# Twelve of the 24 gate blocks as seven half-block products instead of eight, and their activation sums on GpSimd, in a hybrid decoder step

## The reference, cut to what matters

```python
u = rms_norm(x, lp['norm_g'][0])
nq, nkv, ngate, sz, sxbc, sdt, dqkv, mg = split_in(u @ lp['w_in'])
...
gates = jax.nn.sigmoid(mg.reshape(B, T, 3, D_MODEL).astype(jnp.float32)).astype(x.dtype)
mix = (gates[:, :, 0] * o_a + gates[:, :, 1] * o_b + gates[:, :, 2] * o_cc) @ lp['w_out']
```

## Time and profile before

| | us |
|---|---|
| median of 3 runs (lowest, highest) | 3270.55 (3268.74, 3283.62) |
| the profiled execution, its own time | 3274.83 |
| its span from the first to the last instruction | 3273.0 |
| state space stage, gate products and scan | about 1006 to 1311 |
| prompt attention stage: head and transposes of keys and queries | 1311 to 1362 |
| prompt attention stage: the 32 steps | 1362 to 1854 |

### The profile page before, as it was taken

One profiled execution on the slowest core, in us unless ns is written; L12 is line 12 of the kernel. 1 busy time (PEld: TensorE's weight loads), 2 busy tenths in 40 slices (PEclk: granted clock), 3 DMA queues, 4 the chain that ended last, 5 costly groups with the idle time before them and its releaser, 6 DMA issues. The chain is left out here.

```text
span 3273.0 us, 42944 instructions
## 1 busy us (share of the span) xinstructions
PE 3015.6 (92%) x15198; PEld 2004.1 (61%) x15198; DVE 1257.5 (38%) x2963; ACT 640.6 (20%) x1529; POOL 469.3 (14%) x351
## 2 busy tenths in 40 slices
PE   7999999989997899699899899899699999989998
PEld 5777777665555565454554565455488888874443
DVE  3111123225642675255555343133456656550000
ACT  2111000002220333233333221144311111110000
POOL 0001000004301432100000100011122332220000
PEclk8999999999998889899999999899799999999999
DMA  7544253428854432621110444200143333404010
GB/s 171 118 95 103 75 166 112 146 84 231 254 160 129 147 103 65 181 69 36 40 32 33 142 138 156 94 15 33 55 141 110 121 136 108 141 22 158 34 34 26
DMA packets 336639, 344.79 MB, mean 105 GB/s; under 512 B 60945, under 2 KB 305361, under 8 KB 335078
## 3 DMA queue, kind: packets, MB, share of 16 engines
q1 hardware_dynamic: 296730, 262.54, 27.6%
q10 hardware_dynamic: 39734, 79.98, 7.2%
HBM read 289.11 MB, written 110.01 MB: 122 GB/s over the span
## 5 line engine op out<-in xcount | busy, mean ns | idle before, releaser
L284 PE MATMUL d_ps<-d_w,mixer_u_T 128*128 128x288 f32 (+2 forms) x2048 | 610.8, 437 | 15.9 <-PEq L145 10.3
L284 PEld LDWEIGHTS d_ps<-d_w,mixer_u_T 128*128 128x128 f32 x2048 | 375.4, 195 | 150.4 <-issue 47.9
L288 PE MATMUL d_ps<-mixer_u_T,d_w 128*128 128x352 f32 x1152 | 428.9, 498 | 24.4 <-ACT d_ob L308 13.8
L2923 PE MATMUL down_ps<-down_w,feed_g_T 128*128 128x512 f32 x704 | 305.4, 596 | 8.4 <-DMA down_w<-ffn_w_down 8.4
L288 PEld LDWEIGHTS d_ps<-mixer_u_T,d_w 128*128 128x128 f32 x1152 | 206.4, 199 | 131.8 <-issue 70.1
L2923 PEld LDWEIGHTS down_ps<-down_w,feed_g_T 128*128 128x128 f32 x704 | 134.4, 191 | 177.7 <-issue 168.5
L3133 PE MATMUL ffn_ps<-up_u_T,up_up_w 128*128 128x264 f32 x704 | 165.2, 394 | 6.3 <-DMA ffn_state<-state_ffn_conv 6.3
L3133 PE MATMUL ffn_ps<-up_u_T,ffn_S 128*128 128x264 f32 x704 | 163.8, 386 | 0.0
L3133 PE MATMUL ffn_ps<-ffn_T,up_up_w 128*128 128x264 f32 x704 | 163.8, 386 | 0.0
L308 DVE COPY d_ob<-d_ps 128x288 f32<-128x288 f32 (+3 forms) x144 | 66.4, 462 | 233.0 <-PE d_ps L284 158.3
L3133 PEld LDWEIGHTS ffn_ps<-up_u_T,up_up_w 128*128 128x128 f32 x704 | 133.8, 193 | 29.5 <-issue 6.7
(11 more groups left out here) (467 smaller groups left out, 3783.0 us busy)
## 6 DMA issues: line engine op xcount, KB each, us to landing
out_dil_sample<-cache_dil_w ACTq DMA_DIRECT2D x10, 3264.0 KB
up_up_w<-ffn_w_up SPq DMA_DIRECT2D x44, 512.0 KB, 5.1
cmp_rows<-cache_nsa_kv SPq DMA_DIRECT2D x128, 128.0 KB
graw<-d_ob SPq DMA_DIRECT2D x72, 176.0 KB
mix_gate<-graw SPq DMA_DIRECT2D x24, 528.0 KB, 6.0
dils_qb<-proj SPq DMA_DIRECT2D x24, 512.0 KB, 6.9
d_w<-w_in SPq DMA_DIRECT2D x24, 512.0 KB, 5.4
ssd_x<-proj SPq DMA_DIRECT2D x29, 384.0 KB, 4.8
```

Source lines behind the costliest of these rows:

```text
L284: mm = pe.matmul(self.ps[u % 2][0:rows, 0:cols], self.u_T[:, k, r0:r0 + rows], self.view(i)[:, k, :], start=(k == 0), stop=(k == DK - 1))
L288: mm = pe.matmul(self.ps[u % 2][:, 0:cols], self.view(i)[:, k, x, :], self.u_T[:, k, c * third:(c + 1) * third], start=(k == 0), stop=(k = ...
L2923: mm = pe.matmul(ps[i % ring][:, 512 * h:512 * (h + 1)], lhs_T[:, k, r0:r0 + m], w[:, k, 512 * h:512 * (h + 1)], start=(k == 0), stop=(k = ...
```

## The change

Six of the twelve gate parts (the first twelve blocks, `PLAIN`) stay as they are and run in the state space stage. The other twelve blocks are done in the prompt attention stage by the new class `Gates`, two blocks (a pair) at a time. The weights of a pair are a matrix of 2 by 2 halves A (row: block, column: half of the 1024 inputs), the activations one of 2 by 2 halves B (row: half of the inputs, column: half of the tokens), and the four half results come from seven products P1 to P7 (the scheme of Winograd and Strassen) instead of eight. Each product is made in two quarters x = 0, 1 of 264 tokens, 4 instructions of TensorE each, into `ps[x]`.

- T0 to T2, sums over the activations (three matrices of 4 x 528 columns), are made once, by 6 instructions of GpSimd in the state space stage (`sums_lane`, from 0.4 to 0.9 of the stage). The fourth, B12, is made in place in `u_T` by VectorE at the start of the attention stage (2 instructions).
- S2, S3, S4 and A21 + A22, sums over weights, are made by 4 instructions of GpSimd for every pair.
- ScalarE copies P1 out (`kept`), VectorE makes all the sums of results from `ps` (14 additions a pair), 8 of them the results that are stored.
- To make room, three tiles of the state space stage and `raw` of the attention stage now lie in other tiles, the square's unused result goes to `yout`, and `oa` has 2 slots instead of 4, with a wait for the store of two heads before.

```diff
+class Gates:
+    ORDER = [(p, x) for p in ("P1", "P2", "P6", "P7", "P5", "P4", "P3") for x in range(2)]
+    RING = 4
...
+        def pool_program(pool):
+            yield
+            for x in range(2):
+                pool.tensor_tensor(self.T_of(0, x), self.B(0, 1, x), self.B(0, 0, x), ALU.subtract).then_inc(self.T_made, 1)
+                yield
+                pool.wait_ge(self.T_made, 3 * x + 1)
+                pool.tensor_tensor(self.T_of(1, x), self.B(1, 1, x), self.T_of(0, x), ALU.subtract).then_inc(self.T_made, 1)
+                yield
+                pool.wait_ge(self.T_made, 3 * x + 2)
+                pool.tensor_tensor(self.T_of(2, x), self.B(1, 0, x), self.T_of(1, x), ALU.subtract).then_inc(self.T_made, 1)
+                yield
...
+        last_reader = dict(P6="C11", P7="U", P5="W", P4="V", P3="C21")
+        def pe_program(pe):
+            for i in range(pairs):
+                pe.wait_ge(self.w_in[i % 2], 32 * (i // 2 + 1))
+                for p, x in ORDER:
+                    if p == "P2":
+                        pe.wait_ge(self.held, 2 * i + x + 1)
+                    elif p != "P1":
+                        pe.wait_ge(self.summed, self.added(i, last_reader[p], x))
+                    elif i:
+                        pe.wait_ge(self.summed, self.added(i - 1, "C12", x))
+                    if p in S_needed:
+                        pe.wait_ge(self.S_made, 4 * i + S_needed[p])
...
+                    for k in range(KH):
+                        mm = pe.matmul(self.ps[x][:, 0:self.quarter], lhs(i)[:, k, :], rhs(x)[:, k, :], start=(k == 0), stop=(k == KH - 1))
...
+                dve.tensor_tensor(out, base, self.ps[x][:, 0:self.quarter], ALU.add).then_inc(self.summed, 1)
...
+        def pool_program(pool):
+            for i in range(pairs):
+                pool.wait_ge(self.w_in[i % 2], 32 * (i // 2 + 1))
+                if i:
+                    pool.wait_ge(self.product, NP * i)
+                pool.tensor_tensor(self.S(3), self.A(i, 0, 0), self.A(i, 1, 0), ALU.subtract).then_inc(self.S_made, 1)
...
-                act.copy(oa[:, r, i * P:(i + 1) * P], O[s % 2][:, :]).then_inc(out_made, 1)
+                if r >= 2 and i == 0:
+                    act.wait_ge(stored, 16 * (r - 1))
+                act.copy(oa[:, r % 2, i * P:(i + 1) * P], O[s % 2][:, :]).then_inc(out_made, 1)
...
+        PLAIN = 12
+        parts += [("gate", q, P) for q in range(0, PLAIN, 2)]
...
-            ssd(nc, ins, outs, proj, y_b, ident, [(dense.lane(36, settle=False), 0, 1)])
-                together(nc, (dense.lane(36), 0, 1), (nsa_prompt_lane(nc, own, ins, proj, kc_T, vc, oa_T, ident), 0.08, 0.92),
+                ssd(nc, ins, outs, proj, y_b, ident, [(dense.lane(3 * PLAIN, settle=False), 0, 1), (halves.sums_lane(), 0.4, 0.5)])
+                    together(nc, (halves.lane(), 0, 1), (nsa_prompt_lane(nc, own, ins, proj, kc_T, vc, oa_T, ident), 0.08, 0.92),
```

More of the change, by code:

```diff
@@ L328, in sp_program @@
                     self.load(sp, i + 1)
+                elif j == 1:
+                    sp.wait_ge(self.product, self.first[i])
+                    self.behind(sp)
                 if u > lo:
@@ L553, in nsa_prompt_lane @@
     WP = CX + NCMP_P + 1
-    raw = st.sb("raw", [P, 4, 4, P])
     q_T = st.sb("q_T", [P, NSA_R, SEQ])
@@ L569, in nsa_prompt_lane @@
     rs = st.sb("rs", [P, 3, KVH, 3])
-    oa = st.sb("oa", [P, NSA_R, SEQ])
+    oa = st.sb("oa", [P, 2, SEQ])
+    raw = oa[:, :, :].rearrange("p r c -> p (r c)").rearrange("p (i t c) -> p i t c", i=4, c=P)
     S = [st.ps(f"S{g}", [P, 512]) for g in range(KVH)]
@@ L869, in sp_program @@
                 sp.wait_ge(out_made, PT * r)
-                sp.dma_start(oa_T[r - 1], oa[:, r - 1, :]).then_inc(stored, 16)
+                sp.dma_start(oa_T[r - 1], oa[:, (r - 1) % 2, :]).then_inc(stored, 16)
             for _ in range(subs(s)):
@@ L873, in sp_program @@
         sp.wait_ge(out_made, n)
-        sp.dma_start(oa_T[NSA_R - 1], oa[:, NSA_R - 1, :]).then_inc(stored, 16)
+        sp.dma_start(oa_T[NSA_R - 1], oa[:, (NSA_R - 1) % 2, :]).then_inc(stored, 16)
         sp.wait_ge(stored, 16 * NSA_R)
@@ L1438, in ssd @@
         yout = st.sb("yout", [P, 2, SIN])
-        junk = st.sb("junk", [P, SIN])
         ss = st.sb("ss", [P, 4])
@@ L1443, in ssd @@
         h0 = st.sb("h0", [P, DB, NH2 * SP])
-        new = st.sb("new", [P, 2, NH2 * SP])
-        last_rows = st.sb("last_rows", [P, 2, SG * SN])
+        new = sz[:, :].rearrange("p (i c) -> p i c", i=2)
+        last_rows = skip[:, 1, 0:2 * SG * SN].rearrange("p (q n) -> p q n", q=2)
         TS = st.ps("TS", [P, 512])
@@ L1781, in act_chunk @@
             act.wait_ge(y_steps, n * 3 + 3)
-            act.activation(junk[0:m, :], y[0:m, :], ACT.Square, accum_out=ss[0:m, 0:1]).then_inc(squared, 1)
+            if n >= 2:
+                act.wait_ge(stored[n % 2], s_count(n, n % 2))
+            act.activation(yout[0:m, n % 2, :], y[0:m, :], ACT.Square, accum_out=ss[0:m, 0:1]).then_inc(squared, 1)
             act.wait_ge(meaned, n + 1)
@@ L1919, in last_act @@
                 act.wait_ge(s_turned, b + 1)
+                if b == DB:
+                    act.wait_ge(y_steps, 3 * CH - 1)
                 act.copy(h_raw[:, b] if b < DB else last_rows[:, :, :], R[b % 2][:, 0:2, :]).then_inc(s_copied, 1)
@@ L3981, in decoder_step @@
         parts += [("proj", C_Z + i * ((C_DIL - C_Z) // 4), (C_DIL - C_Z) // 4) for i in range(4)]
-        parts += [("gate", q, P) for q in range(0, 3 * DK, 2)]
+        PLAIN = 12
+        parts += [("gate", q, P) for q in range(0, PLAIN, 2)]
         with Stage(nc, "d") as d_st:
             dense = Dense(nc, d_st, u_T, ins, proj, graw, parts)
+            halves = Gates(nc, d_st, dense, ins, graw, PLAIN)
+            dense.behind = lambda sp: halves.load(sp, 0)
             with Stage(nc, "front") as own_f, Stage(nc, "cmp") as own:
@@ L3998, in decoder_step @@
                                                   (scores, 0.05, 0.66), (values, 0.3, 0.67))
-            ssd(nc, ins, outs, proj, y_b, ident, [(dense.lane(36, settle=False), 0, 1)])
-            with Stage(nc, "nsap") as own:
-                together(nc, (dense.lane(36), 0, 1), (nsa_prompt_lane(nc, own, ins, proj, kc_T, vc, oa_T, ident), 0.08, 0.92),
-                         (branch_weights_lane(nc, own, proj, o_dil, lse, gates), 0.3, 0.3),
-                         (copies_lane(kept + moves, moved), 0, 1))
+            with Stage(nc, "gate_sums") as own_g:
+                halves.open(own_g)
+                ssd(nc, ins, outs, proj, y_b, ident, [(dense.lane(3 * PLAIN, settle=False), 0, 1), (halves.sums_lane(), 0.4, 0.5)])
+                with Stage(nc, "nsap") as own:
+                    together(nc, (halves.lane(), 0, 1), (nsa_prompt_lane(nc, own, ins, proj, kc_T, vc, oa_T, ident), 0.08, 0.92),
+                             (branch_weights_lane(nc, own, proj, o_dil, lse, gates), 0.3, 0.3),
+                             (copies_lane(kept + moves, moved), 0, 1))
     with Stage(nc, "feed") as part:
```

144 lines of the change are left out of this document (added).

## The result

The changed kernel takes 3284.19 us (median of 20 runs, 3275.33 to 3291.08), the kernel before on the same chips 3272.96 us (20 runs). The ratio is 1.0031, 95% interval 1.0023 to 1.0039: about 10 us slower, where 2.4 us faster was forecast. The profiled execution has a span of 3289.2 us, and it is about the stages that it speaks. The code ahead of the state space stage is the same in every kernel here, and yet that stage began between 1000.4 and 1021.1 us in the profiled executions.

A forecast was written before the change was run, and what follows sets the result against it. TensorE bounds the attention steps, loads the head. Attention gains 22.2 - 2.8 - 4.0 - 5 - 1 = 9.4 us, the state space stage loses 7: 3270.55 - 2.4 = 3268 us, range 3252 to 3285.

The forecast's parts named there:

- Less work for TensorE, 22.2 us, of it 18.4 in the steps: Attention stage: 288 gate products become 336 narrower ones, 171.4 us become 149.2; 18.4 us saved in the 32 steps.
- the 672 records expected: Sign in the profile after: the gate products' group should have 672 records in the attention stage.
- The head: 2.8 of 3.8 us given up: Attention stage before the first scores: 3.8 us saved on products, but it waits for raw rows, so 1 us kept.
- 4.0 us lost to waits for the maximum: 32 steps: in 44 of some 200 pieces TensorE then waits for VectorE's maximum, so shorter products only lengthen waits; 4.0 us.
- Additions ahead of the weighting, 5 us: 32 steps: VectorE's additions delay its weighting, stalling TensorE in six more steps at 0.8 us: 5 us, bounds 0 and 10.
- When GpSimd's sums meet VectorE's weighting, some collide: 1 us.: Attention stage: some of GpSimd's sums over weights collide with VectorE's weighting, costing 1 us.
- State space stage, +7 us: GpSimd's six sums over activations hold VectorE's work: 6.0 us, plus 1 us of low clock; range 0 to 15.
- 3.3 were counted: State space chunks 4 and 5: sums 2 and 3 each make `E` 1.65 us later, lengthening TensorE's wait by 3.3 us.
- Sums 4 and 5, counted at 0.5 us each: State space stage: these sums fall where `E` was made before and delay the state's decay by 0.5 us each.
- Nearly all of it arrives: Rival, whole kernel: sums hide in GpSimd's idle time, little saving is lost; about -17 us, 3253 us; chance 0.17.
- VectorE's turn: Rival, attention stage: TensorE's 72 accumulator changes wait for VectorE's additions; at 0.45 us average lateness 3300 us; chance 0.13.
- The clock pulled down in later chunks: Rival, state space stage: sums 4 to 6 make new waits, each with a low-clock stretch; +13, 3281 us; chance 0.13.

The follow-up runs named there:

- the fair pair: Kernel before plus GpSimd's scaling waiting for a weighting, 3270.26 us; against changed kernel with GpSimd's weight sums and scaling waiting, activation sums on VectorE, 3258.12 us.
- the experiment: Changed kernel without GpSimd's six sums over activations in the state space stage, unsummed halves used instead: 3271.52 us, ratio 0.9986 to the kernel before.
- the placement on VectorE: Changed kernel with the six sums over activations made by VectorE at the attention stage's head instead of GpSimd: 3277.06 us, ratio 0.9995 to the kernel before.
- the timeline with the scaling: Changed kernel with weight sums after the weighting, activation sums on VectorE in the head, and additions two product turns later: 3259.25 us, ratio 0.9939 to kernel before.

## Why the prediction was wrong, by its own steps

- **Less work for TensorE, 22.2 us, of it 18.4 in the steps.** Right: 18.6 us by the last pair of windows, at clocks of 0.98 and 0.99, so a little of it is the clock. The profile after has the 672 records expected.
- **The head: 2.8 of 3.8 us given up.** Right in kind: the head is 1.6 us shorter, where 1 was expected.
- **4.0 us lost to waits for the maximum.** Not seen. They were to grow to 44 us; they are 38.1, and 39.4 against 39.6 in the fair pair. 18.6 became 15.2 all the same: in the fair pair TensorE's waits for the weighting grew from 2.9 to 5.0 us and its wait for ScalarE's copy from 0.3 to 1.6, together the 3.4 us.
- **Additions ahead of the weighting, 5 us.** Open. Moving them shortened the steps by 1.7, 2.8 and 4.6 us in the three pairs of kernels that differ in this alone, and the medians by 4.7, 8.5 and 10.1 (only the middle pair on one chip; the intervals of each pair's ratios overlap). The first two step differences are about as large as profiled executions differ by themselves. Waits for the weighting fell by 0.2, 0.2 and 0.6 us, so the way I reasoned, through that wait, is not shown. By that wait the additions cost at most the 2.1 us of the fair pair.
- **"When GpSimd's sums meet VectorE's weighting, some collide: 1 us." This is the step that failed.** They cost 12.4 us of the steps, and 15.4 when put into the old kernel. I had the lock's price in the state space rows and did not carry it to this stage. I took it for a matter of VectorE instructions with two SBUF inputs; the weighting has one. The groups that I read gave no sign: in the steps of the kernel before GpSimd works for 13.45 us only the earlier trace rows, in two places, and the weighting of the earlier trace rows is in neither. There a four-column instruction took 3.27 us. I did not follow GpSimd's order either, in which the scaling now stands behind a pair's sums. And I priced a late weighting at its own length, where the clock behind it cost TensorE 7.1 us beside the 9.4 of waits.
- **State space stage, +7 us.** The mechanism was right, the size not: 11.5 us (12.5 by the experiment, 12.1 by the placement on VectorE). `xw` took 2.89 to 2.91 us beside sums 2 to 5, near the 3.2 worked out. The waits for `E` grew by 5.1 us, where 3.3 were counted, those for the state by 1.7, and TensorE's busy time by 3.6. Sums 4 and 5, counted at 0.5 us each, hold `xw` for 1.4 us each like the others. Against the kernel with these sums on VectorE, counted from the stage's start, TensorE's chunk work is late by 2.5 us behind sum 2, 4.1 behind sum 3, 5.2 behind sum 4, 6.8 behind sum 5 and 10.7 at the last chunk; so sums 4 and 5 cost about 1.1 and 1.6 us. VectorE's busy time grew by 11.9 us (171.8 to 183.7), 1.3 of them an instruction of the next stage.
- **The rivals.** "Nearly all of it arrives" (17 us) is false for this kernel. Once GpSimd's work is placed in both kernels, the 7 to 15 us of the fair pair come nearer to it without showing it. "VectorE's turn" is excluded by 0.8 us of waits. "The clock pulled down in later chunks" did happen, at part of its price. After:

```profile
1220.00:1250.00 30.00, 25.16 (x111) 16.14 (x111) 25.05 (x29) 9.27 (x19) 16.93 (x11) 0.94 0.25 76
1250.00:1280.00 30.00, 24.44 (x100) 14.90 (x99) 23.67 (x29) 13.21 (x26) 11.89 (x10) 0.89 0.08 28
```

The kernel before has a clock of 1.00 in both windows. Over the whole stage the difference is small, 0.89 against 0.90.

The result lies in the range for the wrong reason: the range's upper end stood for the clock in the state space stage, and the larger miss, 10.8 us, was in the steps (8.4 shorter by the terms above, 2.4 longer measured), against 4.5 in the state space stage. The forecast had the wrong sign, and the runs could tell: the interval of the ratio is 0.16% wide, where I had counted 0.5% (16 us) as the least that can be seen.

The Trainium skill, page "SBUF — State Buffer", section on the two sides of the memory, names a second case beside two SBUF inputs: VectorE instructions in a two-port performance mode. Under "Who interferes with whom" it counts `tensor_scalar` among those that can enter it. The prediction quoted the half with two inputs and left this half out. The traces agree as far as they go: the weighting and the four-column instruction are `tensor_scalar`, and in the timeline with the scaling the first weighting and the four-column instruction ended within 0.1 us of GpSimd's. Which mode they ran in no row shows.

## What to carry to other kernels

Idle time of GpSimd is not free for VectorE: before work is given to it, list VectorE's instructions in the same stretch, and look at what they last where GpSimd already works. If an instruction of four columns takes 3 us in one place and 0.17 in all others, the price is there to be read. Place such work by what must not be disturbed (here: after a named weighting, or on VectorE itself where TensorE waits for loads) and look at what stands behind it in the queue. And price a wait on a nearly full TensorE with the slow stretch behind it, which here was about as large as the wait. Look beyond the wait for the held instruction, too: a hold can arrive through a third engine.

## What the runs showed of the hardware that I had not expected

- The hold goes by whole instructions also for very small ones: 128x4 took 3.27 us beside a GpSimd instruction of 3.37 us, and 0.17 alone.
- Between GpSimd instructions that follow each other closely, VectorE gets one in, and is held by the next: six weightings of 1.69 us took 4.53 beside sums of 1.27 us each, 2.84 us more (one by one, in order: 0.98, 0.22, 1.46, 1.45, 0.41 and 0.41 us). Beside a scaling instruction of 3.4 us six smaller ones took 3.99 instead of 1.42 us, 2.57 more. So a row of short sums is no gentler than one long instruction.
- Not every VectorE instruction is held: in the timeline with the scaling at 1489.54 the reciprocal of 6 columns took 0.19 us at 1493.01, inside the second scaling, and a bias instruction with 384 columns, which reads TensorE's result `S`, took 0.55 us at 1489.96, inside the first. Both last as long elsewhere.
- One difference of 1056 columns takes VectorE 1.25 us, GpSimd 2.40 to 2.87.
